# The head of a one-layer decoder kernel, written anew

## The reference, cut to what matters

```python
xn = rmsnorm(h, attn_norm)          # h * rsqrt(mean(h*h)) * attn_norm
proj = xn @ w_in                    # 2048 x 22592
q, k, v, z, a, b, sB, sC, sh, gA, gB = jnp.split(proj, IN_SPLITS, axis=-1)
qkv, new_qkv = causal_dwconv(jnp.concatenate([q, k, v], axis=-1), s_qkv, qkv_conv_w)
beta = jax.nn.sigmoid(b)
g = -jnp.exp(a_log) * jax.nn.softplus(a + dt_bias)   # decay, 32 heads
o, S = gated_delta_rule(q, k, v, g, beta, s_gdn)     # needs exp of the running sum of g
```

## Time and profile before

| | |
|---|---|
| runs | 2629.5, 2635.35, 2638.07 us (median 2635.35) |
| the profiled execution's own time | 2622.89 us |
| its span, first to last instruction | 2621.2 us |
| PE busy | 2552.1 us, 97% |
| DVE busy | 1663.2 us, 63% |
| ACT busy | 1317.4 us, 50% |
| POOL busy | 532.3 us, 20% |
| moved by DMA | 507.36 MB, 194 GB/s on average |

### The profile page before, as it was taken

The page is one execution under the profiler, slowest core; times in us unless marked ns, Lnnn a source line. Parts: engine busy times, 40 slices in busy tenths (PEclk is TensorE's granted clock), DMA queues, the critical chain, the costliest instruction groups (busy, mean ns, idle before and its releaser), DMA issues.

```text
span 2621.2 us, 50472 instructions
## 1 busy us (share of the span) xinstructions
PE 2552.1 (97%) x20849; PEld 2526.6 (96%) x20849; DVE 1663.2 (63%) x2866; ACT 1317.4 (50%) x2015; POOL 532.3 (20%) x913
## 2 busy tenths in 40 slices
PE   6989999999999999999999999999999999999997
PEld 5989999999999999999999999999999999999997
DVE  4848676776867675533355566466676656776665
ACT  5536455564646554433344344455565545555653
POOL 1335271725536270000000000100110000100100
PEclk9999999999999999999999999999999999999998
DMA  5545564655556455667655556757986667986563
GB/s 181 169 142 162 150 187 129 181 148 166 157 157 181 138 179 163 196 205 213 203 175 177 187 187 208 242 180 229 315 292 217 220 197 242 311 279 196 166 206 109
DMA packets 444773, 507.36 MB, mean 194 GB/s; under 512 B 21193, under 2 KB 423762, under 8 KB 441858
## 3 DMA queue, kind: packets, MB, share of 16 engines
q1 hardware_dynamic: 416128, 415.42, 50.9%
q0 software_dynamic: 27840, 88.53, 11.0%
q10 hardware_dynamic: 578, 0.19, 0.0%
HBM read 478.15 MB, written 26.49 MB: 193 GB/s over the span
## 4 chain that ended last, share of the span: by engine, by line
PE 61%; POOL 1%; DMA 1%; DVE 1%; issue 0%; ACT 0%; DVEq 0%; POOLq 0%; ACTq 0%
PE bank L692 60%; DMA raw<-in_w_ffn_down 1%; POOL prod L547 1%; POOL sol L550 1%; DVE wlo L1291 0%; PE bank L717 0%; ACT whi L979 0%; DVE xlo L1326 0%; DVEq L225 0%; DMA DT<-sol_scratch 0%; DMA sol_scratch<-sol 0%; POOL sol_scratch L580 0%; POOL DT L584 0%; DVE yrow L1729 0%; DVE yrow L1346 0%
## 5 line engine op out<-in xcount | busy, mean ns | idle before, releaser
L692 PE MATMUL bank<-xhi,whi 128*128 128x264 f32 x5520 | 1592.1, 288 | 10.6 <-DVE wlo L1291 10.6
L692 PE MATMUL bank<-xlo,whi 128*128 128x264 f32 x5520 | 1567.9, 284 | 0.0
L692 PE MATMUL bank<-xhi,wlo 128*128 128x264 f32 x5520 | 1565.9, 284 | 0.0
L1291 DVE TENSOR_TENSOR wlo<-raw,whi 128x1024 fp32r<-128x1024 f32 x828 | 1012.9, 1232 | 729.7 <-ACT whi L979 729.3
L979 ACT ACTIVATE whi<-raw 128x1024 fp32r<-128x1024 f32 x828 | 872.8, 1058 | 797.9 <-PE bank L692 710.5
L692 PEld LDWEIGHTS bank<-xhi,whi 128*128 128x128 f32 x5520 | 1041.4, 189 | 13.5 <-issue 12.8
L692 PEld LDWEIGHTS bank<-xlo,whi 128*128 128x128 f32 x5520 | 1041.8, 189 | 2.2 <-issue 1.9
L692 PEld LDWEIGHTS bank<-xhi,wlo 128*128 128x128 f32 x5520 | 1038.5, 188 | 0.0
L692 PE MATMUL bank<-ahi,whi 128*128 128x264 f32 x704 | 200.1, 284 | 1.7 <-DVE wlo L1291 1.7
L692 PE MATMUL bank<-ahi,wlo 128*128 128x264 f32 x704 | 200.1, 284 | 0.0
L692 PE MATMUL bank<-alo,whi 128*128 128x264 f32 x704 | 199.7, 284 | 0.0
(11 more groups left out here) (293 smaller groups left out, 1843.4 us busy)
## 6 DMA issues: line engine op xcount, KB each, us to landing
raw<-in_w_in SPq DMA_DIRECT2D x356, 512.0 KB, 3.8
raw<-in_w_ffn_gate SPq DMA_DIRECT2D x88, 512.0 KB, 5.7
raw<-in_w_ffn_up SPq DMA_DIRECT2D x88, 512.0 KB, 4.6
raw<-in_w_ffn_down SPq DMA_DIRECT2D x96, 384.0 KB, 3.4
raw<-in_w_gdn_out SPq DMA_DIRECT2D x64, 512.0 KB, 3.4
chunkS<-in_state_gdn POOLq DMA_DIRECT2D x16, 1024.0 KB, 7.3
raw<-in_w_sconv_out SPq DMA_DIRECT2D x32, 512.0 KB, 3.4
raw<-in_w_o SPq DMA_DIRECT2D x32, 512.0 KB, 4.5
```

The costliest lines, as they stand in the source:

```text
L692: return pe.matmul(out, lhsT, rhs, start=start, stop=stop)
L1291: dve.tensor_tensor(wlo[:, at_ % SPLIT, :, :], raw[:, at_ % RAW, :, :], f32(whi[:, at_ % SPLIT, :, :]), ALU.subtract).then_inc(lo_ready, 1)
```

## The change

The head is put in another order.

- **Input by columns.** x is loaded in four column parts of 512, each with its own semaphore, behind a small load of the first gain (`arow`). SP thus issues 13 transfers before piece 0. PE runs 12 matmuls of `ident` by itself, turns `arow` (16 columns), and then turns x as the parts land; it doesn't wait for the other constants.
- **Two engines copy.** DVE copies the even tiles, ACT the odd ones, each with a semaphore. Splits of pieces 0 to 2 stand between the tiles: on ACT behind tiles 5, 8, 11, on DVE behind 6, 9, 12.
- **Norm sums by rows.** ACT squares x as it was loaded, three instructions of 2048 columns with a summed output (`xsum`), behind pieces 0 to 2. DVE puts the sums on diagonals (`xdiag`) behind piece 2, and PE sums them into all partitions with three matmuls behind piece 3 (`row_sums`). The 16 squares and 32 matmuls of `norm_sums` are gone.
- **Constants at piece 3.** The other constants are turned behind piece 3 (`turn_vec`) and copied by DVE there; the convolution states are turned behind pieces 4, 5 and 6, and copied by ACT behind 5, 6 and 7.
- **Decay in stages.** The evacuation of "ab" ends with ln. DVE's scan stands behind the split of piece 8 (j = 5), ACT's three exps behind that of piece 9 (j = 6), DVE's diagonals behind that of piece 10 (j = 7).
- **Steps of group 0.** `kk` and `kcopy` come one piece earlier (j = 10), `exponents` two (j = 10), `exps` and `lt` two (j = 11).
- **POOL.** The store of `hpro` waits for piece 8 and stands behind the broadcast of the decay; the two state copies stand behind group 0.

The diff, cut to its core:

```diff
-    sqr = at("sqr", [P, DTL, N], F32, regO + size([P, DTL, N], F32))
+    sqr = at("sqr", [P, D], F32, regO + size([P, DTL, N], F32))
...
-                   "first": {7: ("kk",)}}
+                   "first": {6: ("kk",)}}
...
-                    "first": {7: ("kcopy",), 9: ("exps",)}}
+                    "first": {6: ("kcopy",), 7: ("exps",)}}
...
-                    "first": {8: ("exponents",), 9: ("lt",)}}
+                    "first": {6: ("exponents",), 7: ("lt",)}}
...
 def _(sp):
-            for b in range(BLK):
-                sp.dma_start(xrow[:, b, :], I["x_prompt"][0, b * P:(b + 1) * P, :]).then_inc(x_in, 16)
-            sp.dma_start(xrow[0:NB, BLK, :], I["x_sample"][:, 0, :]).then_inc(x_in, 16)
+            sp.dma_start(arow[:, :], I["attn_norm"][0].rearrange("(t p) -> t p", p=P)).then_inc(x_in[0], 16)
+            for q in range(4):
+                c = slice(512 * q, 512 * q + 512)
+                for b in range(BLK):
+                    sp.dma_start(xrow[:, b, c], I["x_prompt"][0, b * P:(b + 1) * P, c]).then_inc(x_in[q], 16)
+                sp.dma_start(xrow[0:NB, BLK, c], I["x_sample"][:, 0, c]).then_inc(x_in[q], 16)
...
 def _(pool):
             decay_rows(0)
+            pool.wait_ge(h_copied, DTL // 2)
+            pool.wait_ge(h_copied_odd, DTL // 2)
+            pool.wait_ge(piece_used, 8)
+            pool.dma_start(hT_d, hpro[:, :, :].rearrange("p k t -> p (k t)")).then_inc(h_stored, 16)
             group(0, True, False)
+            pool.dma_start(O["qkv_s"][0, :, 0:2, :], ...).then_inc(states_shifted, 16)
+            pool.dma_start(O["sc_s"][0, :, 0:1, :], ...).then_inc(states_shifted, 16)
...
 def _(pe):
+            def row_sums():
+                pe.wait_ge(diag_ready, 1)
+                for b in range(BLK):
+                    mm(bank[4][:, b * P:(b + 1) * P], ones[:, :], xdiag[:, b, :])
+                mm(bank[4][:, T:N], ones[0:NB, :], xdiag[0:NB, BLK, 0:NB]).then_inc(sum_ready, 1)
...
-                if ph.name == "first" and j < 4:
-                    turn_states(j)
+                if ph.name == "first" and j == 3:
+                    turn_vec()
+                if ph.name == "first" and 4 <= j < 7:
+                    turn_states(j - 4)
+                if ph.name == "first" and j == 6:
+                    turn_states(3)
...
+                    for _ in range(12):
+                        mm(bank[7][:, 0:P], ident[:, :], ident[:, :])
+                    pe.wait_ge(x_in[0], 16 * (BLK + 2))
+                    pe.transpose(bank[7][:, 0:DTL], arow[:, :], ident[0:DTL, 0:DTL]).then_inc(vec_turned, 1)
                     for kt in range(DTL):
+                        if kt % 4 == 0 and kt > 0:
+                            pe.wait_ge(x_in[kt // 4], 16 * (BLK + 1))
+                        if kt == 7:
+                            pe.wait_ge(vec_ready, 1)
                         if kt >= 8:
-                            pe.wait_ge(h_copied, kt - 7)
+                            pe.wait_ge(h_copied if kt % 2 == 0 else h_copied_odd, (kt - 8) // 2 + 1)
...
 def _(act):
+            def decay_rows():
+                act.wait_ge(g_ready, 1)
+                act.activation(prep[R, 8, 0:NB], prep[R, 4, T:N], ACT.Exp)
+                act.activation(prep[R, 5, 0:T], Gc[:, :], ACT.Exp)
...
                     if ph.name == "first":
-                        for kt in range(4 * j, 4 * j + 4):
-                            act.activation(sqr[:, kt, :], hpro[:, kt, :], ACT.Square).then_inc(sq_ready, 1)
+                        if j < BLK + 1:
+                            r = P if j < BLK else NB
+                            if j:
+                                act.wait_ge(sq_ready, j)
+                            act.activation(sqr[0:r, :], xrow[0:r, j, :], ACT.Square, accum_out=xsum[0:r, j:j + 1]).then_inc(sq_ready, 1)
...
+                        if kt % 2 == 1:
+                            act.wait_ge(x_turned, kt + 1)
+                            act.activation(hpro[:, kt, :], bank[kt % 8][:, 0:N], ACT.Copy).then_inc(h_copied_odd, 1)
+                            act.wait_ge(h_copied_odd, kt // 2 + 1)
+                        else:
+                            act.wait_ge(h_copied, kt // 2 + 1)
                         act.activation(xhi[:, kt, :], hpro[:, kt, :], ACT.Copy, scale=vec[:, 304 + kt:305 + kt]).then_inc(xhi_ready, 1)
-                    for p in range(AHEAD):
-                        split(16, p, p + 1)
+                        if kt in (5, 8, 11):
+                            p = (kt - 5) // 3
+                            split(16, p, p + 1)
...
 def _(dve):
+                    if psum and kt in (6, 9, 12):
+                        p = (kt - 6) // 3
+                        split(p, p + 1)
...
+                if ph.name == "first" and j == 3:
+                    dve.wait_ge(vec_turned, 2)
+                    dve.tensor_copy(vec[:, 0:304], bank[5][:, 0:304])
+                    dve.tensor_copy(vec[:, 320:369], bank[5][:, 320:369]).then_inc(vec_ready, 1)
+                elif ph.name == "first" and j == 2:
+                    for b in range(BLK + 1):
+                        r = P if b < BLK else NB
+                        dve.wait_ge(sq_ready, b + 1)
+                        m = dve.tensor_scalar(xdiag[0:r, b, 0:r], ident[0:r, 0:r], xsum[0:r, b:b + 1], None, ALU.mult)
+                    m.then_inc(diag_ready, 1)
+                elif ph.name == "first" and j == 5:
+                    decay_scan()
+                elif ph.name == "first" and j == 7:
+                    state_diagonals()
```

More of the change, by code:

```diff
@@ L512, in _ @@
             sts = I["state_short_conv"][0].rearrange("b j n -> (b j) n")
-            pool.wait_ge(x_in, 16 * (BLK + 1))
+            for q in range(4):
+                pool.wait_ge(x_in[q], 16 * (BLK + (1 if q else 2)))
             for q in range(4):
@@ L883, in extra @@
                     m.then_inc(d_turned, 1)
-                elif ph.name == "first" and j < 4:
-                    norm_sums(range(4 * j, 4 * j + 4))
+                elif ph.name == "first" and j == 3:
+                    row_sums()
                 elif ph.name in ("ffn0r", "pgate") and j == 2:
@@ L892, in extra, with turn_vec @@
                     mm(bank[7][:, 0:256], ones[:, :], so[:, 3, :, :].rearrange("p a b -> p (a b)")).then_inc(so_sum, 1)
+            def turn_vec():
+                pe.wait_ge(v_in, 16 * 10)
+                pe.wait_ge(h_copied, DTL // 2)
+                pe.wait_ge(h_copied_odd, DTL // 2)
+                for i in range(3):
+                    r = 113 if i == 2 else P
+                    m = pe.transpose(bank[5][:, i * P:i * P + r], vrow[0:r, i, :], ident[0:r, 0:r])
+                m.then_inc(vec_turned, 1)
             def turn_states(batch):
@@ L1187, in extra @@
                         act.activation(phi[:, k, :], bank[5 + k][:, 0:N], ACT.Copy).then_inc(xhi_ready, 1)
-                if ph.name == "first" and 1 <= j < 5:
-                    b = j - 1
+                if ph.name == "first" and j == 6:
+                    decay_rows()
+                for b in ((j - 5,) if j in (5, 6) else (2, 3) if j == 7 else ()) if ph.name == "first" else ():
                     nu = min(5, DTL - 5 * b)
@@ L1302, in copy @@
                 def copy(kt):
+                    if kt % 2 == 1:
+                        return
                     dve.wait_ge(x_turned, kt + 1)
@@ L1466, in conv, with decay_scan, state_diagonals @@
                                 m.then_inc(done, 1)
+            def decay_scan():
+                R = slice(0, 32)
+                dve.wait_ge(soft_in, 1)
+                dve.wait_ge(soft_ready, 1)
+                mine.inc(dve.tensor_scalar(prep[R, 1, :], prep[R, 1, :], 0.0, None, ALU.max))
+                mine.inc(dve.memset(prep[R, 7, :], 1.0))
+                dve.wait_ge(ea_ready, 1)
+                mine.inc(dve.tensor_scalar(prep[R, 10, 2:3], prep[R, 10, 3:4], -1.0, None, ALU.mult))
+                mine.settle(dve)
+                mine.inc(dve.tensor_tensor(prep[R, 1, :], prep[R, 1, :], prep[R, 2, :], ALU.add))
+                mine.settle(dve)
+                mine.inc(dve.tensor_scalar(prep[R, 4, :], prep[R, 1, :], prep[R, 10, 2:3], None, ALU.mult))
+                mine.settle(dve)
+                for c in range(NCH):
+                    t = slice(c * CH, (c + 1) * CH)
+                    m = dve.tensor_tensor_scan(Gc[:, t], prep[R, 7, t], prep[R, 4, t], 0.0, ALU.mult, ALU.add)
+                m.then_inc(g_ready, 1)
+            def state_diagonals():
+                R = slice(0, 32)
+                dve.wait_ge(rows_ready, 1)
+                I32 = ident[R, 0:32]
+                dve.tensor_scalar(dgs[:, 0, :], I32, prep[R, 5, T - 1:T], None, ALU.mult)
+                for b in range(NB):
+                    dve.tensor_scalar(dgs[:, 1 + b, :], I32, prep[R, 8, b:b + 1], None, ALU.mult)
+                    m = dve.tensor_scalar(dgs[:, 1 + NB + b, :], I32, prep[R, 3, T + b:T + b + 1], None, ALU.mult)
```

(2 more changed lines are left out.)

83 lines of the change are left out of this document (23 added, 60 removed).

## The result

The changed kernel takes 2609.55 us (median of 4, 2608.11 to 2612.62) beside 2635.11 for the kernel before (4 runs). The ratio is 0.9908, 95% interval 0.9894 to 0.9922: 25.6 us faster, between 20.6 and 27.9. On another chip it was 0.9909 (0.9895 to 0.9923). The forecast was 2612.

What follows compares the result with a forecast made beforehand. PE, busy 97% of the span, was taken as the bound, with group 0's DT chain ending the head. DT at 134.5 instead of 157.7 gains 23.2 us: 2635.35 less 23.2 is 2612, range 2601 to 2626.

Steps and rivals of the forecast that it cites:

- Input: Start of the head: first 512 columns of x landed at 4.8 us, bounds 4.5 and 10.7; extra transfers cost nothing.
- Rival B: Start of the head: first columns land late, at 10.6; 17.4 us gained, 2618; chance 0.16.
- Turn and copy: Conversion of x: ACT starts at 6.7, queues hold each other up by 2.5 us (0 to 4), ACT ends at 24.5.
- Norm sums: Row squares on ACT at 2.1 us each, done at 33.7; diagonals and three matmuls take 1.2, to 34.9.
- Mean, root, decay: Behind the row sums: mean from 36.6, root to 39.4, decay 5.75 us to 45.1; piece 7 starts at 48.
- "lt": DVE's stretch to finished Tt: 25.1 us of work and 4.5 idle (0 to 9), ending at 75.7 instead of 98.9.
- POOL: Chain from finished Tt through the solve to DT kept at 58.8 us; moved store and state copies cost nothing.
- Later groups: Groups behind the head: they keep their order and their waits.
- the sign that I had named for a wrong prediction: Later groups: the prediction is wrong as a whole if PE's waits for DT grow there.
- both cost nothing: POOL: the hT store moved behind piece 8 and the state copies behind group 0 cost nothing; without cover 1.8 us.
- a piece has three others ahead of it: Weight reloads beside the moved store may land later, but each piece has three others ahead of it.
- the 7.0 us hole of PE: PE's wait for a low half at 60.7, in front of piece 7; it was to go, piece 7 starting at 48.

Runs made afterwards that it cites:

- no_warm: The changed kernel without the twelve matmuls of ident ahead of x; ratio 0.9915 to the kernel before.
- before_again: The kernel before, unchanged, profiled once more; one run, 2633.79 us.
- after_same: The changed kernel, unchanged, run once more beside three others on one chip; ratio 0.9909 to the kernel before.
- old_conv: The changed kernel with all 16 copies out of PSUM by DVE and the first three splits behind the conversion; ratio 0.9915 to the kernel before.
- decay_one: The changed kernel with scan, exponentials and diagonals of the decay back in the evacuation of "ab"; ratio 0.9915 to the kernel before.
- best3: The changed kernel without the twelve matmuls, with ACT's table fetched early, fewer diagonal instructions, earlier per-token copies and four reordering edits; ratio 0.9875 to the kernel before.

## Why the prediction was right, point by point

The forecast (23.2 gained, 2612) holds, and so does its mechanism: "the gain at the end of the head is the time by which 'lt' comes earlier". The terms:

- *Input.* The first columns were to be there at 4.8, with 10.7 as the late bound; no_warm shows 6.5. It is hidden in any case: I overlooked that the twelve matmuls hold PE to 7.28, though the diff shows them. ACT's table load starts at 8.66 instead of 6.7, and this step is 2.0 late. Rival B had 10.6 for the columns; moving at 138 GB/s, which the Trainium skill ("DMA: Bandwidth & Descriptors", section "Bandwidth") gives for 64 KB, is not what the case's 256 KB parts did: 275 to 302 GB/s between 4 and 10 us in four traces, all transfers taken together, beside 347 in before_again.
- *Turn and copy.* "I take 2.5" for the queues' holds: ACT waits 1.22, 0.27 and 1.22 for DVE's copies in after_same, 2.7. From the table's end to the start of split 3 it takes 16.1 us, 16.5 were reckoned. But the step treats the copies on ACT as part of the gain's path without asking what they cost there: old_conv shows 1.8.
- *Norm sums.* Third square at 34.6 for 33.7 forecast, row sums at 34.99 for 34.9, with 4.4 idle in front where I had 7. The squares take 1.9 plus the read of the sum, 0.19; I had 2.1.
- *Mean, root, decay.* The mean begins at 37.30 (36.6 forecast), the root ends at 40.0 (39.4, though my terms add up to 39.2), split 7 starts at 45.68 (45.1). The lateness of the start has shrunk to 0.6 here. Piece 7 starts at 49.5 (48).
- *"lt".* 25.1 of work and 4.5 idle were forecast. In after_same DVE is busy 25.0 us of the 30.9 from 47.00 to 77.90, so 5.9 idle, of which the lower clock of PE at `kk`, a term that I had not reckoned with, makes up some 1.25. "lt" ends at 77.69 for 75.7, late mostly by this and by the 0.6 above.
- *POOL.* The chain from "lt" to the use of DT took 59.96 for 58.8. The solve is 36.65 (90.01 to 126.66), group 0's length and not group 1's 39.5. The rule of the Trainium skill ("SBUF — State Buffer", section "SBUF: two separate sides") that I held 3.5 us for was not needed; no run separates the port from other causes. The sum was 23.2; the head gains 20.1 in the first pair and 21.6 in the second. It is too large by the late start and the clock at `kk` (2.0 together at "lt") and by the chain (1.2).
- *Later groups* "keep their order and their waits": their waits for DT sum to 10.7 us in the first trace of before, 16.3 in its second, 15.8, 14.7 and 10.0 in three of after. That growth is not the change's, and the sign that I had named for a wrong prediction must be read against a second trace of before.
- *Where a cause was missed.* Of the store and the copies I wrote "both cost nothing", and of the reloads beside the store that "a piece has three others ahead of it". The first was true of the new place and said nothing of the old one; the second was wrong there: with them in the way ACT waited 7.06 us for a weight piece (7.08 in before_again). The row lay in ACT's timeline, between the two of the earlier trace rows that I showed. My sum came out right all the same, since it follows the new queues from the start and has no wait for a transfer in it. I also led with the 7.0 us hole of PE; decay_one shows that the hole stays away without the staging of the decay, by which I had closed it, and that the staging is worth nothing that shows in the time.

Open: the median gains 25.6 and 23.4 us on two chips, the traces of the head 20 to 21.6. The lower ends of the intervals are 20.6 and 20.2, so no place need be sought for the rest, and none was found. That 2612 lies as near as 2.4 us to the median is in part luck: the head gained less than my sum, the median more. And why the granted clock at `kk` falls in some traces and not in others is not shown.

## What to carry to other kernels

Follow the one chain that ends last (here "lt", then some 54 us through POOL) and price each edit by what it does to that chain alone; holes of another engine ahead of the same wait are paid out of it. When a transfer is moved, look for who waited beside its old place: its worth here was a weight reload that landed in 4.7 instead of 10.0 us. Before sharing work with a second engine, ask whether that engine carries the chain: ACT did here, and the copies cost it 1.8 us up to the first square. And before a mark of one execution is put down to an edit, compare the granted clock along the chain: a step of it moved "lt" by 1.25 us.

## What the runs showed of the hardware that was not expected

Behind twelve matmuls without a pause a tile of x is turned in 0.52 us; without them, or after 3.6 us of idleness, in 0.82. The record of the granted clock shows 0.50 for the last case and 1.00 for the one without them, with the same 0.82: so early in a run the pitch of the instructions tells the level of the clock (1.2 GHz) and the recorded 1.00 does not. At `kk` the length of the wait in front doesn't tell the level: behind 2.8 to 3.1 us the three traces of the changed kernel show a granted 0.50 there, behind 3.2 in no_warm it is 1.00. In best3 PE waits 1.7 us for DT and the stretch behind it shows a granted 1.00, where the kernel after, behind 4.4, shows 0.50 for 5.65 us:

```profile
137.65:139.00 1.35, 1.35 (x6) 1.35 (x7) 0.00 (x0) 0.00 (x0) 1.35 (x3) 0.50 0.90 315
139.00:143.30 4.30, 4.30 (x22) 4.30 (x21) 1.29 (x2) 0.16 (x1) 4.30 (x10) 0.50 0.07 11
```

```profile
128.00:134.00 6.00, 4.52 (x39) 4.55 (x40) 1.29 (x2) 1.54 (x2) 6.00 (x13) 1.00 0.62 181
```
